# A hybrid attention layer on one core: scores negated at their source, rope DMAs and k copies reordered on ScalarE, top-k halves moved

## The chip, the core and the metric

The kernel runs on one core of one Trainium2 chip. Its time is the device time of one execution in microseconds (us); three executions of the kernel before gave 364.44, 366.65 and 367.55 us, median 366.65. Five engines run side by side and meet only at semaphores: TensorE (PE in the profile), VectorE (DVE), ScalarE (ACT), GpSimd (POOL) and SyncE (SP), which here only issues DMAs. ACT issues DMAs too; those rows are marked ACTq.

## What is computed

One decoder layer over 16 meta tokens and 512 others, so 528 positions, width 1024. All of it is float32.

```python
h = layer_norm(concat(meta, x))
qa, ka, va, ga, qi, ki, wi, cq, ckv, kpe, gb = split(h @ w_in)
# branch A: an indexer scores keys, the best 128 per row stay, 8 heads of 64
idx = sum_h relu(qi_h @ ki.T * scale_i) * wi_h ; sel = top_k(idx, 128)
la = qa @ k_sel.T * scale_a + bias[distance] ; oa = softmax(la) @ v_sel
# branch B: low-rank q and kv, 8 heads of 64, plus 32 rotary columns
q_nope, q_pe = rms(cq) @ w_uq ; k_nope, vb = rms(ckv) @ w_ukv
lb = (q_nope @ k_nope.T + rope(q_pe) @ rope(kpe).T) * scale_b, causal
ob = softmax(lb) @ vb
out = concat(oa * silu(ga), ob * silu(gb)) @ w_out
y = layer_norm(ALPHA * h + out)
```

A softmax subtracts each row's maximum before the exponential.

## The kernel before

The program is written out by hand. The function schedule() makes one list, ORDER, of stages, and each of the five engine programs walks that same list in order and does its own part of each stage. So a stage's place in the list sets its place on every engine that has work in it, and an engine never overtakes itself.

The weights come from HBM in blocks of 128 columns (raw). Stage W n makes a block's high part on ACT (wh, line 508) and its low part on POOL or DVE (wl, line 501); PE then multiplies in three passes (high by high, high by low, low by high). SP loads the raw block n+3 when the low part of block n is done. A stage J is one such product, a job, and writes one of two PSUM banks in turn: job j may start when job j-2 has been copied out. Jobs named in the steps: qn p and kn p (the 64 non-rotary columns of q and k of head pair p of branch B; kn comes in two halves), va (v of branch A), qa p and ka p (q and k of branch A; ka in two halves), tq g (three of the transposes of head g), out (the output projection).

Heads are numbered g = 0 to 15; 0 to 7 are branch B, 8 to 15 are branch A. For each head:

- S g: PE writes the scores of four row tiles into PSUM in two units, and DVE finds each row's maximum (mx; line 1025, for branch A line 1027, which also adds the bias). DVE then multiplies three, and later one, of these maxima by minus the scale (nm, line 1033).
- X g: ACT does four exponentials with bias nm (line 798), each of which also gives the row sum.
- R g: DVE takes the reciprocals, POOL scales the rows.
- TP g and tq g: PE transposes the probabilities of head g; these stages come inside head g+1.
- PV p: PE multiplies by v for a pair of heads.

In branch B, each pair's q_b holds 64 copied rows and 32 rotary rows. The rotary rows were computed earlier for all heads (qpe), and two DMAs of 64 KB, issued by ACT right behind its copy of q_b, bring them in (line 716). PE waits for both before S of the pair's first head (qpe_in). ACT's copies of kn and ka out of PSUM are lines 720 and 739; DVE's parts of them are lines 931 and 937.

The top-k is 14 rounds of two halves each (pick() puts them into ORDER as TOPK r half): a long half over the row tile of 512 keys and a short one over the three smaller tiles. DVE does them between other work of heads 0 to 7. After the last of them DVE makes the mask (MASK), and then copies qa 0 out (line 909).

## Time and profile before

| what | value |
|---|---|
| median of three runs | 366.65 us |
| lowest, highest | 364.44, 367.55 us |
| profiled execution, its time | 364.95 us |
| its span in the trace | 363.1 us |
| PE busy | 335.2 us (92%) |
| DVE, ACT, POOL busy | 241.4, 173.8, 160.2 us |
| granted TensorE clock, mean | 0.996 |

The time of an execution is the span plus what lies around it, here 1.85 us. "Idle before" in a row is how long that engine stood still before the instruction, and what ended the wait. A matmul's end is modelled, so its start is the better mark; a gap on PE is a wait that a row names.

### The profile page before, as it was taken

The page shows a single profiled execution, that of the slowest core. Times are in us where ns is not written, and L with a number is a line of the kernel's source. Part 1 is how long each engine was busy: PE and PEld are TensorE (multiplying, and loading weights), DVE is VectorE, ACT ScalarE, POOL GpSimd, SP SyncE. Part 2 cuts the span into 40 slices and gives each one's busy share as a digit, 9 for nine tenths or more (in the row PEclk, how much of TensorE's full clock was granted, in tenths as well). Part 3 has the DMA queues.
Part 4 walks back from the last instruction along what each step waited for, and adds up shares of the span by engine and source line. Part 5 has one row for each costly group of instructions (what it writes and reads, how often), then busy time and mean ns, then how long its engine had stood idle before and what let it go on. Part 6 is the DMA issues. An engine that isn't in the chain of part 4 may idle for free.

```text
span 363.1 us, 6163 instructions
## 1 busy us (share of the span) xinstructions
PE 335.2 (92%) x2155; PEld 277.1 (76%) x2155; DVE 241.4 (66%) x654; ACT 173.8 (48%) x382; POOL 160.2 (44%) x140
## 2 busy tenths in 40 slices
PE   1699999999999979999999999999989899999991
PEld 1488887888788748886968877887868688987981
DVE  5762221297766989888986796667767775533566
ACT  4674644542743354557344554654666542622230
POOL 3342999766341612346304450742233222550464
PEclk9999999999999999999999999999999999999998
DMA  7463433249211231013000140421312220130023
GB/s 265 157 214 138 133 108 104 81 170 290 69 60 58 86 105 58 16 58 116 18 16 0 60 146 3 145 89 58 92 28 89 88 81 11 58 117 0 2 116 118
DMA packets 11566, 32.87 MB, mean 91 GB/s; under 512 B 2392, under 2 KB 2392, under 8 KB 11536
## 3 DMA queue, kind: packets, MB, share of 16 engines
q1 hardware_dynamic: 8944, 27.08, 21.8%
q10 hardware_dynamic: 2592, 5.40, 4.9%
q8 instruction: 18, 0.29, 0.4%
q14 instruction: 12, 0.10, 0.1%
HBM read 29.83 MB, written 4.81 MB: 95 GB/s over the span
## 4 chain that ended last, share of the span: by engine, by line
PE 69%; DVE 10%; ACT 8%; issue 7%; DMA 2%; POOL 2%; SPq 0%; ACTq 0%; DVEq 0%; POOLq 0%
PE ps_j L1153 44%; PE ps_s L1342 5%; PE ps_o L1393 5%; PE ps_s L1309 2%; ACT pr L798 2%; DMA res<-in_x 2%; POOL wl L501 2%; PE ps_j L1195 2%; DVE pr L1027 2%; PE ps_t L1363 1%; ACT ks L739 1%; ACT wh L508 1%; PE ps_s L1350 1%; PE ps_t L1368 1%; PE ps_j L1206 1%
## 5 line engine op out<-in xcount | busy, mean ns | idle before, releaser
L501 POOL TENSOR_TENSOR wl<-raw,wh 128x1024 fp32r<-128x1024 f32 (+2 forms) x33 | 77.3, 2348 | 92.8 <-ACT wh L508 92.7
L1153 PE MATMUL ps_j<-hh,wh 128*128 128x512 f32 (+2 forms) x224 | 79.4, 354 | 1.4 <-DVE qs L909 1.3
L1153 PE MATMUL ps_j<-hl,wh 128*128 128x512 f32 (+2 forms) x224 | 77.8, 347 | 0.0
L1153 PE MATMUL ps_j<-hh,wl 128*128 128x512 f32 (+2 forms) x224 | 77.7, 347 | 0.0
L631 POOL TENSOR_SCALAR pr<-pr,rden 128x528 f32<-128x528 f32 (+1 forms) x64 | 33.7, 546 | 60.8 <-DVE rden L1042 60.8
L1153 PEld LDWEIGHTS ps_j<-hh,wh 128*128 128x128 f32 (+1 forms) x224 | 41.9, 187 | 11.0 <-issue 5.5
L1153 PEld LDWEIGHTS ps_j<-hh,wl 128*128 128x128 f32 (+1 forms) x224 | 41.8, 187 | 5.4
L1153 PEld LDWEIGHTS ps_j<-hl,wh 128*128 128x128 f32 (+1 forms) x224 | 41.8, 187 | 5.4 <-issue 0.2
L508 ACT ACTIVATE wh<-raw 128x1024 fp32r<-128x1024 f32 (+2 forms) x35 | 35.9, 1039 | 4.4 <-DMA raw<-in_weights 2.8
L1153 PE MATMUL ps_j<-wh,hh 128*128 128x256 f32 (+1 forms) x112 | 32.1, 286 | 2.4 <-ACT k_b L720 1.3
L1153 PE MATMUL ps_j<-wl,hh 128*128 128x256 f32 (+1 forms) x112 | 31.4, 280 | 0.0
L1153 PE MATMUL ps_j<-wh,hl 128*128 128x256 f32 (+1 forms) x112 | 31.3, 280 | 0.0
L798 ACT ACTIVATE pr<-pr,nm 128x528 f32<-128x528 f32 (+3 forms) x32 | 18.0, 564 | 22.5 <-DVE nm L1033 22.5
L798 ACT ACTIVATE pr<-ps_s,nm 128x528 f32<-128x528 f32 (+3 forms) x32 | 16.9, 540 | 19.5 <-DVE nm L1033 19.5
L996 DVE MATCH_REPLACE8 iw<-top,iw 128x512 f32<-128x512 f32 (+3 forms) x56 | 26.2, 475 | 0.0
L992 DVE MAX8 top<-iw 128x8 f32<-128x512 f32 (+3 forms) x56 | 24.5, 478 | 0.0
L1153 PEld LDWEIGHTS ps_j<-wh,hh 128*128 128x128 f32 (+1 forms) x112 | 19.6, 175 | 4.4 <-issue 2.5
L1342 PE MATMUL ps_s<-k_b,q_b 96*128 96x240 f32 (+4 forms) x80 | 22.2, 404 | 0.0
L909 DVE SCALAR_TENSOR_TENSOR qs<-ps_j,qs 64x512 fp32r<-64x512 f32 x16 | 11.0, 689 | 15.9 <-ACT qs L700 15.6
L980 DVE SCALAR_TENSOR_TENSOR iw<-ps_s,wi,iw 128x512 f32<-128x512 f32 (+3 forms) x28 | 13.5, 543 | 10.9 <-ACT ps_s L784 10.8
L1153 PE MATMUL ps_j<-wh,mbh 128*128 128x256 f32 x64 | 18.7, 292 | 1.4 <-DVE res L946 1.4
L1153 PEld LDWEIGHTS ps_j<-wh,hl 128*128 128x128 f32 (+1 forms) x112 | 19.6, 175 | 0.4
(216 smaller groups left out, 756.0 us busy)
## 6 DMA issues: line engine op xcount, KB each, us to landing
raw<-in_weights SPq DMA_DIRECT2D x37, 512.0 KB, 3.4
bias_by_distance<-bias_vector ACTq DMA_DIRECT2D x1, 2624.0 KB, 13.5
bias<-bias_by_distance ACTq DMA_DIRECT2D x8, 264.0 KB, 3.2
res<-in_x SPq DMA_DIRECT2D x4, 512.0 KB, 5.4
out<-res SPq DMA_DIRECT2D x3, 512.0 KB, 2.8
pt<-in_ln_emb_g SPq DMA_DIRECT2D x1, 512.0 KB, 5.2
pt<-in_ln_emb_b SPq DMA_DIRECT2D x1, 512.0 KB, 6.6
q_b<-qpe ACTq DMA_DIRECT2D x8, 64.0 KB, 2.0
```

The source lines that it names most:

```text
L501: eng.tensor_tensor(ring_of(False, b), raw_of(b), ring_of(True, b).bitcast(F32), ALU.subtract).then_inc(done, 1)
L508: act.activation(ring_of(True, b), raw_of(b), ACT.Copy).then_inc(w_high, 1)
L631: pool.tensor_scalar(a, a, rden[:, k, n:n + 1], 1.0, ALU.mult, ALU.mult).then_inc(scaled, 1)
L798: act.activation(dst, src, ACT.Exp, bias=nm[:, k, n:n + 1], scale=SCALE_B if g < HEADS else 1.0, accum_out=den[:, k, n:n + 1]).then_inc(e_ ...
L909: dve.scalar_tensor_tensor(out=qs[HD:P, n % 2, e, :], in0=bank[HD * e:HD * e + HD, :], scalar=SCALE_A, in1=qs[0:HD, n % 2, e, :].bitcast(F32),
L980: dve.scalar_tensor_tensor(out=iw[:, s], in0=ps_s[:, s], scalar=wi[:, i, h:h + 1], in1=iw[:, s] if h else ci[:, NQ - P * (i + 1):NQ], op0= ...
L992: dve.max(top8[:, i, :], iw[:, IOFF[i]:IOFF[i] + P * (i + 1)]).then_inc(done, 1)
L996: dve.match_replace(out=a, in_to_replace=top8[:, i, :], in_values=a, imm_value=TAKEN).then_inc(done, 1)
L1027: last = dve.tensor_tensor_reduce(pr[:, k, POFF[i]:POFF[i] + NK[i]], src, bias[:, g - HEADS, T - NK[i]:T], 1.0, -3e38, ALU.add, ALU.max, m ...
L1153: last = pe.matmul(dst, a, b, start=n == 0 and part[0], stop=n == count - 1 and part[1])
L1342: pe.matmul(dst, q_b[:, e, i * P:(i + 1) * P], k_b[:, e, a:b], start=True, stop=b <= c0)
L1393: last = pe.matmul(ps_o[HD * e:HD * e + HD, q0:NQ], v[0:r, j, c:c + HD], pt[0:r, e, CO[j]:CO[j] + NQ - q0], start=j == 0, stop=j == 4)
```

## The change

Five things.

1. Scores are negative from the start. The copies of qn, the rotary product and the copies of qa carry a factor of minus the scale, the bias table is negated and the mask value is positive. DVE now finds a row's minimum (mn), which is the exponential's bias as it stands; the exponential's scale is -1. The 32 small multiplications (nm) are gone, and so are the DVE's own waits ahead of them. The semaphores s_max and s_neg become one, s_min, counted per tile.
2. The rotary product's two multiplications by the tables become scalar_tensor_tensor, and DVE's copy of q_b a tensor_scalar.
3. The two rope DMAs of a pair become a stage of their own, QPE p, behind both halves of kn p.
4. The weight block that came right behind qn 0 comes behind va 0 0, the first va job. In heads 9, 11 and 13 the first half of ka comes ahead of X instead of behind it.
5. Top-k halves: one more in heads 2 and 6, and none behind R 7, where there were two.

```diff
-    job("qn", 0)
-    job("kn", 0, 0)
-    job("kn", 0, 1)
+    job("qn", 0, extra=0)
+    job("kn", 0, 0, extra=0)
+    job("kn", 0, 1, extra=0)
+    order.append(("QPE", 0))
...
-        order += [("S", g), ("X", g)]
+        order.append(("S", g))
+        if g > HEADS and g % 2 and more:
+            job(*jobs.pop(0), extra=0)
+        order.append(("X", g))
...
         if g < HEADS and g % 2 == 0:
-            pick(2 if g == 4 else 1)
+            pick(1 if g == 0 else 2)
         if g == HEADS - 1:
-            pick(2)
             assert not halves
...
             job(*j, extra=int(j[0] == "out"))
+            if j[0] == "kn" and j[2]:
+                order.append(("QPE", j[1]))
...
-                        act.activation(q_b[0:HD, 0, :], bank[0:HD, :], ACT.Copy).then_inc(job_act, 1)
-                        act.wait_ge(rope_t, n // 2 + 1)
-                        for e in range(2):
-                            r = 32 * ((2 * n + e) % 4)
-                            act.dma_start(q_b[HD:HD + 32, e, :], qpe[r:r + 32, n // 2, :]).then_inc(qpe_in, 16)
+                        act.activation(q_b[0:HD, 0, :], bank[0:HD, :], ACT.Copy, scale=-SCALE_B).then_inc(job_act, 1)
...
+                elif stage == "QPE":
+                    n = arg[0]
+                    act.wait_ge(rope_t, n // 2 + 1)
+                    if n:
+                        act.wait_ge(s_mm, 4 * n)
+                    for e in range(2):
+                        r = 32 * ((2 * n + e) % 4)
+                        act.dma_start(q_b[HD:HD + 32, e, :], qpe[r:r + 32, n // 2, :]).then_inc(qpe_in, 16)
...
-                        act.wait_ge(s_neg, 2 * g + (1 if n < 3 else 2))
+                        act.wait_ge(s_min, 4 * g + (3 if n < 3 else 4))
...
-                        act.activation(dst, src, ACT.Exp, bias=nm[:, k, n:n + 1],
-                                       scale=SCALE_B if g < HEADS else 1.0,
+                        act.activation(dst, src, ACT.Exp, bias=mn[:, k, n:n + 1], scale=-1.0,
...
-                        dve.tensor_tensor(tmp[:, 1, :], tmp[:, 1, :], sin_sb[:, META:T], ALU.mult).then_inc(rope_m, 1)
+                        dve.scalar_tensor_tensor(out=tmp[:, 1, :], in0=tmp[:, 1, :], scalar=-SCALE_B,
+                                                 in1=sin_sb[:, META:T], op0=ALU.mult, op1=ALU.mult).then_inc(rope_m, 1)
...
-                        dve.wait_ge(s_max, 4 * g + n)
-                        dve.tensor_scalar(nm[:, k, n0:n], mx[:, k, n0:n], -SCALE_B if g < HEADS else -1.0, None,
-                                          ALU.mult).then_inc(s_neg, 1)
```

PE's instructions stand in the same order as before; only the semaphores it waits on carry other names. Three places where the other engines' order changes:

ACT at the first pair (q_b, k_b: q and k of branch B; v_a: v of branch A; wh: a weight block's high part). Before, then of the change:

```order
L712 ACTIVATE q_b<-ps_j 64x512
L716 DMA q_b<-qpe 32x512 x2
L508 ACTIVATE wh<-raw 128x8x128
L720 ACTIVATE k_b<-ps_j 64x264 x2
L727 ACTIVATE v_a<-ps_j 128x256
```

```order
L715 ACTIVATE q_b<-ps_j 64x512
L719 ACTIVATE k_b<-ps_j 64x264 x2
L747 DMA q_b<-qpe 32x512 x2
L726 ACTIVATE v_a<-ps_j 128x256
L511 ACTIVATE wh<-raw 128x8x128
```

The DMAs and the weight block moved behind the k_b copies, the block behind v_a too.

ACT at the second pair, in head 1; heads 3 and 5 have the same. Before, then of the change:

```order
L798 ACTIVATE pr,den<-ps_s,nm 128x400
L712 ACTIVATE q_b<-ps_j 64x512
L716 DMA q_b<-qpe 32x512 x2
L727 ACTIVATE v_a<-ps_j 128x256
L720 ACTIVATE k_b<-ps_j 64x264 x2
L809 ACTIVATE pt<-ps_t 128x512
```

```order
L805 ACTIVATE pr,den<-ps_s,mn 128x400
L715 ACTIVATE q_b<-ps_j 64x512
L726 ACTIVATE v_a<-ps_j 128x256
L719 ACTIVATE k_b<-ps_j 64x264 x2
L747 DMA q_b<-qpe 32x512 x2
L815 ACTIVATE pt<-ps_t 128x512
```

The DMAs moved from the head of the q, v and k copies to their end, ahead of the copies of the transposes (pt).

DVE in head 7, from the row maxima or minima (mx, mn) to the copy of qa 0 (qs); top and iw are the top-k's. Before, then of the change:

```order
L1025 TENSOR_REDUCE mx<-ps_s 128x1
L1033 TENSOR_SCALAR nm<-mx 128x1
L992 MAX top<-iw 128x8 x3
...
L1042 RECIPROCAL rden<-den 128x1
L992 MAX top<-iw 128x8
L996 MATCH_REPLACE iw<-top,iw 128x512
L992 MAX top<-iw 128x8 x3
...
L1002 TENSOR_SCALAR mask<-iw 128x128
...
L909 SCALAR_TENSOR_TENSOR qs<-ps_j,qs 64x512 x2
```

```order
L1033 TENSOR_REDUCE mn<-ps_s 128x1 x4
L1001 MAX top<-iw 128x8 x3
...
L1047 RECIPROCAL rden<-den 128x1
L1011 TENSOR_SCALAR mask<-iw 128x128
...
L915 SCALAR_TENSOR_TENSOR qs<-ps_j,qs 64x512 x2
```

A long and a short half went from between the reciprocals and the mask to heads 2 and 6.

## Rows read from the trace of the kernel before

**Rows 1.** The profile's page: span, and busy time of each engine.

```profile
span 363.1 us, 6163 instructions
PE 335.2 (92%) x2155; PEld 277.1 (76%) x2155; DVE 241.4 (66%) x654; ACT 173.8 (48%) x382; POOL 160.2 (44%) x140
```

**Rows 2.** Waits of PE from 118 us on: total, times, longest.

```profile
PE ps_j L1195 <- ACT ks L739: 2.2, 2, 1.1
PE ps_j L1153 <- DVE res L946: 1.4, 2, 0.7
PE ps_j L1153 <- ACT k_b L720: 1.3, 1, 1.3
PE ps_j L1153 <- DVE qs L909: 1.3, 1, 1.3
PE ps_j L1153 <- DVE q_b L927: 0.7, 1, 0.7
```

**Rows 3.** Timeline (start, us, instruction, idle before) of ACT at the first pair.

```profile
132.75 0.59 ACT L712 ACTIVATE q_b<-ps_j 64x512 f32<-64x512 f32 x1 [1.23 <-PE ps_j L1153]
132.76 1.22 ACTq L716 DMA_DIRECT2D q_b<-qpe  x2
...
135.05 0.64 ACT L720 ACTIVATE k_b<-ps_j 64x264 f32<-64x264 f32 x2
```

**Rows 4.** Timelines of DVE, ACT and PE between S 0 and S 1.

```profile
139.99 0.54 DVE L996 MATCH_REPLACE8 iw<-top,iw 128x384 f32<-128x384 f32 x1
140.67 1.27 DVE L1025 TENSOR_REDUCE mx<-ps_s 128x1 f32<-128x528 f32 x3
...
143.60 0.21 ACT L798 ACTIVATION_READ_ACCUMULATOR pr<-ps_s,nm 128x1 f32 x1
144.12 0.37 PE L1342 MATMUL ps_s<-k_b,q_b 96*128 96x240 f32 x1
```

**Rows 5.** Timelines of ACT and PE at the second pair, up to S 2.

```profile
148.90 0.51 ACTq L716 DMA_DIRECT2D q_b<-qpe  x1
149.44 0.62 ACTq L716 DMA_DIRECT2D q_b<-qpe  x1
152.54 0.38 ACT L720 ACTIVATE k_b<-ps_j 64x264 f32<-64x264 f32 x1 [0.44 <-PE ps_j L1153]
153.79 0.37 PE L1342 MATMUL ps_s<-k_b,q_b 96*128 96x240 f32 x1
```

**Rows 6.** Line 716's DMAs, issue to landing: all eight; the third pair's.

```profile
DMA to landing us min/median/max: 1.9/2.0/3.6
...
DMA to landing us min/median/max: 2.7/2.8/2.9
```

**Rows 7.** Timelines of DVE and ACT around a bias DMA, in head 12.

```profile
275.98 0.15 DVE L1033 TENSOR_SCALAR nm<-mx 128x1 f32<-128x1 f32 x1
276.17 0.33 ACTq L647 DMA_DIRECT2D bias<-bias_by_distance  x1
...
277.13 0.61 ACT L798 ACTIVATE pr<-pr,nm 128x400 f32<-128x400 f32 x1
```

**Rows 8.** Timeline of DVE: idle in head 2, then top-k and mask behind R 7.

```profile
163.25 0.56 DVE L1051 COPY pt<-ps_t 128x384 f32<-128x384 f32 x1 [0.70 <-PE ps_t L1372]
...
211.77 0.67 DVE L992 MAX8 top<-iw 128x8 f32<-128x512 f32 x1
...
215.50 1.04 DVE L1002 TENSOR_SCALAR mask<-iw 128x128 bf16<-128x128 f32 x4
```

**Rows 9.** Timelines of ACT and DVE in head 13: the ka copies.

```profile
286.52 3.24 ACT L739 ACTIVATE ks<-ps_j 64x264 fp32r<-64x264 f32 x8
...
287.40 3.66 DVE L937 TENSOR_TENSOR ks<-ps_j,ks 64x264 fp32r<-64x264 f32 x8 [0.59 <-ACT ks L739]
```

**Rows 10.** Timelines of DVE and POOL in head 14.

```profile
294.72 1.51 DVE L1033 TENSOR_SCALAR nm<-mx 128x3 f32<-128x3 f32 x1
...
293.79 2.41 POOL L501 TENSOR_TENSOR wl<-raw,wh 128x1024 fp32r<-128x1024 f32 x1 [5.31 <-ACT wh L508]
```

More of the change, by code:

```diff
@@ L50 @@
 SCALE_W = HEADS ** -0.5
-MASKED = -float(2.0 ** 100)
+MASKED = float(2.0 ** 100)
 FUTURE = -1e38
@@ L325, in build @@
         ones = sb("ones", [P, P])
-        mx = sb("mx", [P, 2, 4])
-        nm = sb("nm", [P, 2, 4])
+        mn = sb("mn", [P, 2, 4])
         den = sb("den", [P, 2, 4])
@@ L427, in build @@
         s_mm = sem("s_mm")
-        s_max = sem("s_max")
-        s_neg = sem("s_neg")
+        s_min = sem("s_min")
         e_done = sem("e_done")
@@ L487, in slot_free @@
             if SLOT[b] >= RING:
-                eng.wait_ge(s_neg, 4 * HEADS)
+                eng.wait_ge(s_min, 8 * HEADS)
         def high_made(eng, b):
@@ L700, in _ @@
                             act.activation(qs[0:HD, n % 2, e, :], bank[HD * e:HD * e + HD, :], ACT.Copy,
-                                           scale=SCALE_A).then_inc(job_act, 1)
+                                           scale=SCALE_A if kind == "qi" else -SCALE_A).then_inc(job_act, 1)
                     elif kind == "gate":
@@ L753, in _ @@
                         w = (512, VECW - 512)[n]
-                        act.activation(vec_sb[:, 512 * n:512 * n + w], vec_bank(n), ACT.Copy).then_inc(vec_cp, 1)
+                        act.activation(vec_sb[:, 512 * n:512 * n + w], vec_bank(n), ACT.Copy, scale=-1.0).then_inc(vec_cp, 1)
                     act.wait_ge(vec_cp, 2)
@@ L909, in _ @@
                             dve.scalar_tensor_tensor(out=qs[HD:P, n % 2, e, :], in0=bank[HD * e:HD * e + HD, :],
-                                                     scalar=SCALE_A, in1=qs[0:HD, n % 2, e, :].bitcast(F32),
+                                                     scalar=SCALE_A if kind == "qi" else -SCALE_A,
+                                                     in1=qs[0:HD, n % 2, e, :].bitcast(F32),
                                                      op0=ALU.mult, op1=ALU.subtract).then_inc(job_dve, 1)
@@ L918, in _ @@
                         dve.stream_shuffle(tmp[:, 1, :], bank, SWAP).then_inc(job_dve, 1)
-                        dve.tensor_tensor(tmp[:, 0, :], bank, cos_sb[:, META:T], ALU.mult).then_inc(job_dve, 1)
+                        dve.scalar_tensor_tensor(out=tmp[:, 0, :], in0=bank, scalar=-SCALE_B, in1=cos_sb[:, META:T],
+                                                 op0=ALU.mult, op1=ALU.mult).then_inc(job_dve, 1)
                         dve.wait_ge(job_dve, BY_DVE[j + 1])
-                        dve.tensor_tensor(tmp[:, 1, :], tmp[:, 1, :], sin_sb[:, META:T], ALU.mult).then_inc(rope_m, 1)
+                        dve.scalar_tensor_tensor(out=tmp[:, 1, :], in0=tmp[:, 1, :], scalar=-SCALE_B,
+                                                 in1=sin_sb[:, META:T], op0=ALU.mult, op1=ALU.mult).then_inc(rope_m, 1)
                         dve.wait_ge(rope_m, n + 1)
@@ L926, in _ @@
                             dve.wait_ge(s_mm, 4 * n)
-                        dve.tensor_copy(q_b[0:HD, 1, :], bank[HD:P, :]).then_inc(job_dve, 1)
+                        dve.tensor_scalar(q_b[0:HD, 1, :], bank[HD:P, :], -SCALE_B, None, ALU.mult).then_inc(job_dve, 1)
                     elif kind == "kn":
@@ L1020, in _ @@
                         dve.wait_ge(s_mm, 2 * g + u + 1)
-                        n0 = n
                         for i in tiles:
@@ L1024, in _ @@
                             if g < HEADS:
-                                last = dve.tensor_reduce(mx[:, k, n:n + 1], src, AX_X, ALU.max)
+                                last = dve.tensor_reduce(mn[:, k, n:n + 1], src, AX_X, ALU.min)
                             else:
                                 last = dve.tensor_tensor_reduce(pr[:, k, POFF[i]:POFF[i] + NK[i]], src,
-                                                                bias[:, g - HEADS, T - NK[i]:T], 1.0, -3e38,
-                                                                ALU.add, ALU.max, mx[:, k, n:n + 1])
-                            last.then_inc(s_max, 1)
+                                                                bias[:, g - HEADS, T - NK[i]:T], 1.0, 3e38,
+                                                                ALU.add, ALU.min, mn[:, k, n:n + 1])
+                            last.then_inc(s_min, 1)
                             n += 1
-                        dve.wait_ge(s_max, 4 * g + n)
-                        dve.tensor_scalar(nm[:, k, n0:n], mx[:, k, n0:n], -SCALE_B if g < HEADS else -1.0, None,
-                                          ALU.mult).then_inc(s_neg, 1)
                 elif stage == "R":
@@ L1335, in _ @@
                         else:
-                            pe.wait_ge(s_neg, 2 * (g - 1) + u + 1)
+                            pe.wait_ge(s_min, 4 * (g - 1) + (3, 4)[u])
                         for i in tiles:
```

## Prediction, made before the changed kernel ran

> **What bounds the kernel.** I read the page first: PE is busy 335.2 of 363.1 us, no other engine over 66% [rows 1]. So time is gained only where PE stands still, and lost wherever it is made to. The list of PE's waits behind the first 118 us, the stretch that the change touches, is short [rows 2]: 2.2 us for the ka copies, 1.4 us for out copies (0.7 each), 1.3 us for the copy of k_b, 1.3 us for the copy of qa 0, and 0.7 us for DVE's copy of q_b, which the change leaves alone. The 6.2 us of the first four are the ceiling of every gain. PE has no wait at all for a rope DMA, and PE's own order stays. So each part is priced by what it does to a gap of PE; the timelines round each gap show the slack.
>
> **Part 1, the nm multiplications go.** Each stood between a row maximum and the exponential that ACT waits for. Mostly that is not on PE's path. The exception is head 14: one nm took 1.51 us, since it ran beside a POOL subtraction from 293.79 to 296.20 and ended right behind it [rows 10]; undisturbed, an nm takes 0.15 us [rows 7]. Behind it on DVE stand the last maximum and the copy of the first out job, for which PE then waits 0.7 us [rows 2]. About 1.35 us of DVE time goes at that place, more than the gap, so **-0.7**. The second out wait, in head 15, hangs on ACT behind weight copies that follow that head's exponentials; they start about 0.15 us earlier without nm: **-0.15**, with 0 and -0.7 as its ends. The added forms are one-for-one: a scalar_tensor_tensor for a tensor_tensor, a tensor_scalar for a copy, of the same shape and the same PSUM bank. I take 0; no row shows the new pair, and if each q_b copy cost 0.2 us more PE would pay it only at the first pair, where DVE's q_b copy already ends PE's wait of 0.7 us [rows 2]. A fixed scale in an exponential costs what another does: 0.
>
> **Part 2, first pair.** ACT issued two DMAs and made a weight block before it copied k_b, at 135.05 [rows 3]; PE waited 1.3 us for that copy [rows 2]. Now the k_b copy follows the q_b copy, which ended at 133.34, and is done at about 133.7, before PE wants the bank. The 1.3 us go at that spot. What is late next: DVE. Its top-k halves last until 140.53, and it began S 0's maxima at 140.67 [rows 4]; S 0 comes 1.3 us earlier, but DVE does not. The third exponential's sum was read at 143.60 to 143.81 and PE entered S 1 at 144.12 [rows 4], with 0.3 us to spare. Without nm and with the maxima starting at about 140.5, that exponential ends about 0.33 us earlier, at 143.48, and PE, ready at 142.8, must wait until 143.55. So of 1.3 us some 0.75 come back as a wait at S 1: **-0.55**, ends -0.3 and -1.3. The rope DMAs are now issued when kn 0 is done, at 134.4 and 134.95; with 2.0 us to land they are in at 137.0, and S 0 wants them at 137.3. With 3.6 us [rows 6] S 0 would start at 138.6, which the wait at S 1 mostly hides: 0. The weight block (for qn 1) is made 3.6 us later, on ACT, POOL and in SP's next load; PE needs it at about 146, it is done by about 141.5: 0.
>
> **Part 3, the other three pairs.** This is the part that costs. PE's order is kn p, then 1.25 us of transposes, then S: ACT saw the last kn done at 152.54 and PE began S 2 at 153.79 [rows 5]; the two later pairs, in heads 3 and 5, repeat it to within 0.02 us. Before, the DMAs went out at 148.90 and 149.44, over 4 us ahead [rows 5]. Now ACT first waits for kn's last half. The second DMA goes out 0.54 us behind the first, and lands L later, so S starts at 152.54 + 0.54 + L, which is L - 0.71 behind its old place. With L = 2.04 that is 1.33 us, for the second and fourth pair. The third pair's DMAs had 2.7 to 2.9 us, beside a weight load which is still under way at the new place too [rows 6]; I take 2.5, between it and the undisturbed 2.0, so 1.8 us. Sum **+4.5**; ends: L = 1.9 everywhere gives 3.6, L = 3.6 everywhere 8.7. Nothing hides it: PE has no gap worth 0.4 us between 136 and 218 us to give back [rows 2].
>
> Does ACT really hold the DMA until kn is done? The rows on bias DMAs say so: at 276.17 one goes out, with no wait of its own, 0.04 us after the last nm that ACT's queue waits for (275.98 + 0.15) and while its exponentials run on to 277.7 [rows 7]. So a DMA passes running work but no open wait ahead of it; the rope DMAs at 148.90 kept to the same. The Trainium skill states it otherwise (Advanced Engine Details and Errata, Sequencer and Instruction Queues): an engine instruction is pushed into a queue, waits for its semaphores there, and the sequencer reads on. By that rule the DMAs would leave before kn is done, and this part would cost 0. It is the first rival below.
>
> The Trainium skill also gives a local DMA a fixed 2.0 us plus its bytes over 436 GB/s and tells authors to issue early and wait late (DMA: Bandwidth & Descriptors, Anatomy of one DMA, Rules for kernel authors). It speaks against this move; an estimate from that page alone is 2.15 us to land and 4.3 us for the three pairs, where the rows' sum is 4.5.
>
> **Part 4, ka ahead of the exponentials.** In heads 11 and 13 PE waits 1.1 us each to write tq, because the first ka half is copied behind the exponentials: ACT 286.52 to 289.76 for both halves, DVE from 287.40 [rows 9]. In the new place the first half is copied from about 283.2 on ACT and 284.7 on DVE and done by 286.5, while tq comes at 288.2. The exponentials start 0.5 us later, and their scaled rows are wanted one head later: 0. **-2.2**. Head 9 has no such wait: 0.
>
> **Part 5, top-k halves.** Behind R 7 a long and a short half take 211.77 to 215.4 [rows 8], then mask and qa's copy, for which PE waits 1.3 us [rows 2]. With 3.7 us less ahead of it the copy waits for ACT's instead, and is done at about 215.3, before 217.1 when PE wants it: **-1.3**. The halves go to heads 2 and 6, 1.4 us each. DVE stood idle for 0.7 us in head 2 behind its top-k [rows 8], and for more in head 6, and gets at least 0.3 us a head from nm and further time from PE's later S: 0, with +0.3 as the other end. In heads 3 to 5 halves only trade places.
>
> **Sum.** -0.7 - 0.15 - 0.55 + 4.5 - 2.2 - 1.3 = -0.4 us. Against the profiled execution, 364.95 us, that is 364.5. The median of the runs shown is 1.7 us above it; against the median I forecast **366.2 us**: no change that can be measured. About 1%, 3.7 us, is what a measurement of this kernel can tell from no change.
>
> **Rivals.**
> - The DMAs are not held (above). Then part 3 is 0 and the sum is -4.9: **361.8 us**, faster by 1.3%. For it: the Trainium skill's rule. Against it: [rows 7], and the same in the other six bias DMAs without a wait of their own and in the first rope DMA of each later pair: they left 0.04 to 0.13 us behind the last nm. Chance 0.11.
> - More than 3.7 us gained although they are held: the S 1 wait doesn't come, L is 1.9, and gaps below what the list counts close with nm. Ends of the terms: -0.7 - 0.7 - 1.3 + 3.6 - 2.2 - 1.3 = -2.6, and it would take 1.1 us beyond that: 362.5. Chance 0.07.
> - Slower: rope DMAs land late. L was 3.6 us once of eight [rows 6]. If the new places meet weight loads or other transfers, L = 3.6 in each of the three heads makes 8.7 us of part 3, a sum of +3.8: **370.4 us**. It decides from L of about 3.6 us on average; the third pair's 2.8 speaks for it, the 2.0 of two others against. Chance 0.1.
> - DVE becomes the bound in heads 2 to 6 with the halves moved there: the copy of q_b or k_b would come late in three heads by up to 0.7 us, +2: 368.2. It was never waited for there before. Chance 0.04, within 1%.
>
> The forecast, with its smaller variants, has 0.68. Chances: faster by over 1% 0.18, within 1% 0.72, slower 0.10. The range takes in the first rival's edge and the ends of part 3 short of its worst: 362.0 to 369.0.
>
> **What would show it.** In the changed profile, PE's waits should name the rope DMA (q_b<-qpe) three times, at S 2, S 4 and S 6, with 1.3 to 2 us each, and a wait of about 0.7 us at S 1 for ACT's exponential. The waits for ks and qs should be gone, the two for out copies one, and smaller. The rope DMAs should be issued with the last k_b copy of their pair. The forecast is wrong if S 2, S 4 and S 6 show no wait, if those waits pass 2.5 us, or if PE waits for DVE in heads 2 to 6.

## The result, and the profile after

| kernel | median us | lowest, highest | runs |
|---|---|---|---|
| before | 364.97 | 363.74, 367.55 | 20 |
| after | 369.06 | 364.34, 373.53 | 20 |

After over before is 1.0052, 95% interval 1.0028 to 1.0075: slower by half a percent. By the medians it is 4.1 us, 1.1%. The two differ because the ratio leaves out runs over 1.5% above the fastest of their kernel, and the median has all 20. The forecast of 366.2 us was 2.9 us too low, and 369.06 us lies 0.06 us outside its range. Taken as a change it missed by more: -0.4 us was forecast and +4.1 us came. The forecast hung on the median of three executions, 366.65 us, which 20 executions of the same kernel put at 364.97, so the base was 1.7 us too high and hid that much of the miss. The wide spread is the first thing to explain. The runs of the changed kernel stand on steps, and each step has its own granted clock:

| mean granted clock of the run | runs | us | mean |
|---|---|---|---|
| 0.994 to 0.996 | 4 | 364.34 to 365.94 | 365.1 |
| 0.991 | 2 | 366.30, 366.32 | 366.3 |
| 0.985 to 0.987 | 7 | 367.64 to 370.51 | 369.0 |
| 0.977 to 0.978 | 7 | 371.88 to 373.53 | 372.7 |

The kernel before has one such step, and seldom: of its 23 runs in the first comparison below, 19 had a clock of 0.992 or more, and four 0.990, with 367.1 to 367.4 us; none was lower. The changed kernel was at 0.991 or less in 16 of 20. So there are two things to explain: what it costs at full clock (365.1 us, against 364.4, the median of before's 19 runs at 0.992 or more: no change to speak of, as the sum had it), and a loss of clock that comes and goes from run to run.

The profiled execution of the changed kernel took 366.30 us, one of the two at 0.991. Its page, to be held against [rows 1]; the last row shown is the granted clock in 40 slices, in tenths:

```profile
span 364.4 us, 6134 instructions
...
PE 336.8 (92%) x2155; PEld 277.9 (76%) x2155; DVE 231.6 (64%) x622; ACT 173.9 (48%) x382; POOL 160.5 (44%) x140
...
PEclk9999999999999999999999899999999999999998
```

DVE has 32 instructions and 9.8 us less busy time. Those 32 are the nm; they lasted 11.3 us in all, partly side by side with their neighbours. PE has the same 2155 matmuls and yet 1.6 us more busy time: the same products ran more slowly somewhere, and one slice in the middle shows an 8.

PE's waits from 118 us on answer to [rows 2] (us in total, times, longest):

```profile
PE ps_s L1347 <- DMA q_b<-qpe: 5.1, 3, 2.0
PE ps_j L1158 <- ACT k_b L719: 1.1, 2, 0.7
PE ps_j L1158 <- DVE res L959: 1.0, 3, 0.4
PE ps_s L1347 <- ACT v_a L726: 0.5, 1, 0.5
PE ps_j L1158 <- ACT pt L732: 0.4, 1, 0.4
```

All that was to go is gone: ks 2.2, qs 1.3, the 1.3 for k_b, and the 1.4 for out copies but for a 0.4 that now names pt. (The 0.7 in k_b's row is the wait at the first pair that stood as q_b's before, with both copies done at about the same time; its other 0.4 was a wait of 0.2 for v_a. The row for res was there before, with 1.1 us.) What came is 5.1 us for the rope DMAs, in three waits, and 0.5 us at S 0, the row that names v_a; e6_first_pair_alone below says what that is. The sum of all of PE's gaps from 30 us on is 9.1 us in both traces.

Then the stretches of one of these waits, at S 6. Timeline of ACT, to be held against [rows 5] (start, us, instruction, idle before):

```profile
196.43 0.38 ACT L719 ACTIVATE k_b<-ps_j 64x264 f32<-64x264 f32 x1 [0.53 <-PE ps_j L1158]
196.49 1.16 ACTq L747 DMA_DIRECT2D q_b<-qpe  x2
```

The chain of waits through the same place (start, us, what):

```profile
196.49 0.51 ACTq L747
...
197.03 2.07 DMA q_b<-qpe
199.10 0.25 issue
199.34 1.13 PE ps_s L1347 x4
```

And PE's timeline there:

```profile
197.29 0.55 PE L1200 MATMUL ps_j<-ident,pr 128*128 128x128 f32 x3
199.34 1.13 PE L1347 MATMUL ps_s<-k_b,q_b 96*128 96x240 f32 x4 [1.50 <-DMA q_b<-qpe]
...
201.50 1.63 PE L1347 MATMUL ps_s<-k_b,q_b 96*128 96x400 f32 x2
...
203.35 0.41 PE L1158 MATMUL ps_j<-wh,hl 128*128 128x256 f32 x1
...
205.06 0.28 PE L1158 MATMUL ps_j<-wl,hh 128*128 128x256 f32 x1
```

The DMAs leave 0.06 us behind the start of ACT's last k_b copy, not before. The second lands at 199.10, and PE starts S 6 0.25 us later. The 256-column products behind it read 0.41 us at 203.35 and 0.28 us at 205.06: same line, same shape. Busy time by stretch says why (us, then busy time of PE, weight loads, DVE, ACT, POOL, then the granted clock, DMA share, GB/s):

```profile
195.00:199.00 4.00, 2.53 (x21) 1.89 (x20) 3.01 (x11) 2.38 (x7) 0.10 (x1) 1.00 0.13 33
199.00:201.00 2.00, 1.66 (x9) 1.30 (x10) 0.89 (x6) 0.73 (x1) 1.19 (x1) 1.00 0.00 0
201.00:204.00 3.00, 3.00 (x13) 2.06 (x12) 1.98 (x5) 0.89 (x3) 1.15 (x1) 0.51 0.25 63
204.00:206.00 2.00, 2.00 (x17) 2.00 (x16) 1.96 (x8) 1.31 (x6) 0.56 (x1) 0.87 0.45 176
```

PE stood for most of 197.8 to 199.3; from 201.1 to 204.5 it was granted half its clock (1.2 instead of 2.4 GHz). Followed matmul by matmul, S 6 runs 4.5 us later than before, and the products behind the slow stretch 6.1 us later: it cost 1.6 us by itself. In the trace of before the clock falls only at 360.1 us, 4.8 us behind PE's last matmul, where it costs PE nothing:

```profile
355.00:360.00 5.00, 0.27 (x3) 0.07 (x1) 4.47 (x8) 0.29 (x1) 2.87 (x2) 1.00 0.24 96
360.00:365.00 5.00, 0.00 (x0) 0.00 (x0) 0.68 (x2) 0.00 (x0) 0.00 (x0) 0.51 0.31 116
```

All 13 traces end so. Of them the eight with a mean clock of 0.992 or more have no slow stretch ahead of PE's last matmul, and the five with 0.991 or less have one each. So a mean of 0.991 or less is taken below as the sign of a fall; what differs between 0.992 and 0.996 in these traces is only where that last stretch begins.

That is one slow stretch, and it makes one step of the table above. The others fit: a run of span s whose mean clock is d under 0.995 had PE at half clock for 2·s·d longer, and loses half of that, s·d. For 0.986 that is 368 · 0.009 = 3.3 us (measured 369.0 - 365.1 = 3.9), for 0.9775 it is 6.5 us (measured 7.6), for 0.991 it is 1.5 us (measured 1.2). This is an estimate: only one run of this kernel was traced, and the end of the span alone moves the mean by up to 0.004.

### The profile page after: what moved, and what is told of

It reads as the page before. It is cut to its first block, busy times and chain, and to the rows that moved or that the text cites. A ratio compares the mean times of both kernels' runs of the same rounds, so it can differ in the third digit from the quotient of the medians.

```text
span 364.4 us, 6134 instructions
## 1 busy us (share of the span) xinstructions
PE 336.8 (92%) x2155; PEld 277.9 (76%) x2155; DVE 231.6 (64%) x622; ACT 173.9 (48%) x382; POOL 160.5 (44%) x140
## 4 chain that ended last, share of the span: by engine, by line
PE 79%; DVE 5%; DMA 5%; issue 4%; ACT 4%; POOL 2%; SPq 0%; ACTq 0%; DVEq 0%; POOLq 0%
PE ps_j L1158 51%; PE ps_s L1347 6%; PE ps_o L1398 5%; PE ps_s L1355 3%; PE ps_s L1314 2%; DMA res<-in_x 2%; POOL wl L504 2%; DMA q_b<-qpe 2%; PE ps_j L1200 2%; PE ps_t L1368 1%; PE ps_s L1357 1%; PE ps_t L1373 1%; ACT pr L805 1%; PE ps_j L1211 1%; PE ps_j L1216 1%
## 5 line engine op out<-in xcount | busy, mean ns | idle before, releaser
L1347 PE MATMUL ps_s<-k_b,q_b 96*128 96x240 f32 (+4 forms) x80 | 23.5, 422 | 5.6 <-DMA q_b<-qpe 5.1
L805 ACT ACTIVATE pr<-ps_s,mn 128x528 f32<-128x528 f32 (+3 forms) x32 | 16.9, 539 | 20.8 <-DVE mn L1033 20.8
L805 ACT ACTIVATE pr<-pr,mn 128x528 f32<-128x528 f32 (+3 forms) x32 | 18.0, 565 | 10.7 <-DVE mn L1035 10.6
L1033 DVE TENSOR_REDUCE mn<-ps_s 128x1 f32<-128x528 f32 (+3 forms) x32 | 14.1, 501 | 11.0 <-PE ps_s L1351 11.0
```

What stands on the lines that cost most here:

```text
L805: act.activation(dst, src, ACT.Exp, bias=mn[:, k, n:n + 1], scale=-1.0, accum_out=den[:, k, n:n + 1]).then_inc(e_done, 1)
L1033: last = dve.tensor_reduce(mn[:, k, n:n + 1], src, AX_X, ALU.min)
L1347: pe.matmul(dst, q_b[:, e, i * P:(i + 1) * P], k_b[:, e, a:b], start=True, stop=b <= c0)
```

## Where the time went: the rope DMAs

The theory at this point: the parts gain what was forecast, the three waits for rope DMAs take it back at full clock, and PE's standing at those waits is what lets the clock fall. The rival: the clock falls with something else in the changed kernel (the new order of loads, the negated data), and the waits have nothing to do with it.

**e1_rope_early**: the changed kernel with the rope DMAs of the last three pairs back behind the q_b copy. (rope_in(act, n) is a helper with what stage QPE did: its waits and the pair's two DMAs.)

```diff
@@ kind == "qn" on ACT
                         act.activation(q_b[0:HD, 0, :], bank[0:HD, :], ACT.Copy, scale=-SCALE_B)...
+                        if n:
+                            rope_in(act, n)
@@ stage == "QPE" on ACT
-                    n = arg[0]
-                    ...
+                    if arg[0] == 0:
+                        rope_in(act, 0)
```

> The changed kernel with one edit: the rope DMAs of pairs 1 to 3 go out right behind ACT's q_b copy again, as before the change (pair 0 keeps its new place). Theory A (the rope DMAs are held behind kn, PE waits for them at S 2, S 4 and S 6, and the TensorE clock falls to 1.2 GHz behind such a wait in many executions): the three waits (1.57, 1.99, 1.50 us) are gone, and no stretch at half clock is left but the one at the end of the program. Gain over the kernel before = its gaps 9.1 us less the 4.0 that remain = 5.1 us: about 360 us, ratio 0.986, with runs within 2 us of each other. Rival B (the clock falls because of something else in the change, such as the negated scores or the moved top-k): the three waits are gone too, but stretches at half clock stay in most runs, and the runs spread over several us.

Measured: 359.14 us (358.04 to 360.1, 6 runs, all at a clock of 0.993 or 0.994), ratio 0.9841, interval 0.9803 to 0.9879. So this one move turns 4.1 us of loss into 5.5 us of gain. It is 9.9 us faster than the changed kernel, of which the three waits are only 5 to 6. (The two come from different comparisons; each held against its own runs of before, the difference is 9.6 us.) PE's waits from 118 us on:

```profile
PE ps_j L1163 <- DVE res L964: 1.0, 3, 0.4
PE ps_j L1163 <- ACT k_b L729: 0.7, 1, 0.7
```

No wait is over 0.7 us, and the clock does not fall ahead of PE's last matmul. The third pair's second DMA took 3.8 us to land here (166.93 to 170.69), longer than any in the changed kernel, and PE did not wait for it: it had gone out early enough.

**e2_rope_late_alone**: the kernel before, with nothing of the change but these three pairs' DMAs behind kn.

```diff
@@ schedule()
             job(*j, extra=int(j[0] == "out"))
+            if j[0] == "kn" and j[2]:
+                order.append(("QPE", j[1]))
@@ kind == "qn" on ACT (the DMAs of pair 0 stay)
-                        act.wait_ge(rope_t, n // 2 + 1)
-                        for e in range(2): ...
+                        if n == 0: ...
...
+                elif stage == "QPE" and arg[0]: ...
```

> The kernel before with one edit: the rope DMAs of pairs 1 to 3 behind kn. Theory A: three waits of 1.5 to 2.0 us for the rope DMA on PE, 5 to 6 us, less up to 1.3 us that the wait for qa's copy gives back since DVE catches up with the top-k; plus 1.7 us for each stretch of 3.4 us at half clock, none to four in a run. So 369 to 371 us without such a stretch, 370 to 377 us in all. Rival B: 369 to 371 us in every run, with no stretch at half clock.

Measured: 372.03 us (370.12 to 373.24, 6 runs), ratio 1.0191, interval 1.0151 to 1.0231; five of the six runs at a clock of 0.990 or less. The profiled execution:

```profile
PE ps_s L1351 <- DMA q_b<-qpe: 5.8, 3, 2.3
PE ps_j L1204 <- ACT ks L741: 2.1, 2, 1.1
```

5.8 us of waits, and 7.35 us by the medians. Its clock, too, falls behind one of the waits: S 4 starts at 177.21, the half clock begins at 179.0.

```profile
175.00:178.00 3.00, 1.01 (x6) 0.75 (x5) 2.60 (x13) 1.04 (x3) 0.90 (x2) 1.00 0.19 51
178.00:182.00 4.00, 4.00 (x17) 2.75 (x16) 2.31 (x7) 0.89 (x3) 0.00 (x0) 0.63 0.00 0
```

This kernel has none of the negation and none of the other moves. So none of that is needed for the fall. (By the length of the waits alone the run was expected at 369 to 371 us; the one run at 0.992 took 370.12.)

**e4_rope_between**: the changed kernel with the DMAs of the last three pairs between the two halves of kn instead of behind both. Pair 0 keeps its place, though the expectation has all four pairs.

```diff
-            if j[0] == "kn" and j[2]:
+            if j[0] == "kn" and not j[2]:
                 order.append(("QPE", j[1]))
```

> The changed kernel with the rope DMAs behind the first half of kn, ahead of its second (all four pairs). ACT sees the first half of kn done 0.4 to 1.0 us before the second. The wait at S is issue of the first DMA + 0.54 + time to land - start of S, so each of the three waits shrinks by that much, to 0.5 to 1.5 us; sum of the gain 2 to 2.5 us. Theory A: shorter waits let the clock fall less often, so the median gains more than the waits alone: 363 to 365 us. Rival (a DMA does not wait for the copies ahead of it, and the lateness has another cause): the waits stay as they are.

Measured: 365.91 us (362.42 to 370.05, 12 runs), ratio 1.0018, interval 0.9984 to 1.0051; four runs had a clock of 0.992 or more, with 362.4 to 364.4 us; the other eight had 0.988 or less. At S 2 and S 6 PE now waits 0.6 us; at S 4, where the second DMA took 2.5 us to land and not 2.0 or 2.1, it still waits 1.6 us:

```profile
PE ps_s L1347 <- DMA q_b<-qpe: 1.6, 1, 1.6
...
PE ps_s L1347 <- ACT pt L732: 0.6, 1, 0.6
PE ps_s L1347 <- ACT pt L730: 0.6, 1, 0.6
```

The rows of 0.6 us name ACT's copies of pt, but S has no wait for these in the program, and it began 0.24 and 0.25 us behind the second DMA's landing, as in the changed kernel; so these waits are for the DMA too. Against PE's own work the DMAs went out 0.9, 0.4 and 0.9 us earlier. That takes away about half of the waiting (5.1 to 2.8 us) and a third of the loss (3.2 of 9.9 us), and leaves falls in 8 of 12 runs. So it is no remedy for the clock: one wait of 1.6 us was left, and the clock is still unsteady. The next runs test that by itself.

## What makes the clock fall: one wait, filled, or longer

**e3_filler**: the changed kernel with dummy products on PE while it would wait at S 2, S 4 and S 6. The sums are overwritten and nobody reads them. (p is the pair; the wait on e_done makes sure that the previous head's exponentials have read the bank.)

```diff
@@ stage == "S" on PE, ahead of pe.wait_ge(qpe_in, ...)
+                        if p:
+                            pe.wait_ge(e_done, 4 * (g - 1) + 3)
+                            for _ in range(4 if p == 2 else 3):
+                                pe.matmul(ps_s[:, SOFF[3]:SOFF[3] + 240], q_b[0:HD, 0, 3 * P:4 * P],
+                                          k_b[0:HD, 0, 0:240], start=True, stop=True)
```

> The changed kernel with one addition: while PE waits for the rope DMAs at S 2, S 4 and S 6 it runs 3, 4 and 3 products of 64 x 240 on the rows of q_b and k_b that are already there, into the PSUM region that S overwrites next (their results are not used). They take about 1.5, 2.0 and 1.5 us. Theory A: S starts when it did, within 0.5 us, but PE was not idle, so the clock does not fall: all runs at 364.5 to 366.5 us, granted clock at 0.994 or more. If the clock falls because of the sequence of work and not because of PE's idleness, runs spread from 364 to 373 us as those of the changed kernel do.

Measured: 366.11 us (364.35 to 369.47, 12 runs), ratio 1.0034, interval 1.0001 to 1.0067; two of 12 runs at 0.991 or less (369.0 and 369.5 us), where the changed kernel had 16 of 20. S starts no sooner (the ten other runs took 365.8 us on average, the changed kernel's four at full clock 365.1), PE does more work, and the median is 2.9 us lower. At S 2 three products were too few: 0.7 us of wait was left.

**e9_one_wait**: e1_rope_early with one late pair, the third.

```diff
-                        if n:
+                        if n in (1, 3):
                             rope_in(act, n)
...
-                    if arg[0] == 0:
-                        rope_in(act, 0)
+                    if arg[0] in (0, 2):
+                        rope_in(act, arg[0])
```

> e1_rope_early with the rope DMAs of the third pair alone behind the last kn copy: PE waits once, at S 4, for about 2.0 us (as in the changed kernel), at S 2 and S 6 it doesn't. Against e1_rope_early's 359.1 us the wait costs 2.2 us. If PE's clock falls because PE stood at such a wait, at most one stretch of half clock (1.7 to 2 us) is added ahead of the last jobs, and only in part of the runs: the runs lie at 361.3 and 363.1 us, median 361.3 to 363.2. Rival (the clock falls by chance, with PE's high load over the run, whatever the waits): e1's six runs had no fall, so none or as many as the kernel before's (4 of 23), median 361.3. Second rival (three waits are needed, one does nothing): as the rival, no run above 362.5.

Measured: 363.60 us (361.66 to 364.8, 12 runs), ratio 0.9946, interval 0.992 to 0.9972. The three runs at 0.992 or more took 361.66 to 362.13 us, 2.5 to 3 us over e1_rope_early; the nine others, at 0.985 to 0.989, took 362.70 to 364.80. One wait is enough. The median is above the range expected (361.3 to 363.2), since a fall can last longer than 3.4 us: in the profiled execution it lasted 6.8 us and cost 3.2 us. PE there:

```profile
171.75 0.55 PE L1205 MATMUL ps_j<-ident,pr 128*128 128x128 f32 x3
174.16 1.13 PE L1352 MATMUL ps_s<-k_b,q_b 96*128 96x240 f32 x4 [1.86 <-DMA q_b<-qpe]
```

```profile
172.00:174.00 2.00, 0.30 (x3) 0.06 (x1) 1.83 (x8) 1.04 (x3) 0.95 (x3) 1.00 0.29 82
174.00:175.00 1.00, 0.84 (x4) 0.77 (x5) 0.00 (x0) 0.00 (x0) 0.00 (x0) 1.00 0.00 0
175.00:178.00 3.00, 3.00 (x11) 1.76 (x9) 0.93 (x2) 0.00 (x0) 0.00 (x0) 0.57 0.00 0
178.00:182.00 4.00, 4.00 (x19) 3.81 (x18) 3.79 (x15) 2.20 (x8) 0.54 (x1) 0.50 0.00 0
```

**e11_one_wait_filled**: the same kernel, and four dummy products in that one wait. This is the sharpest pair of the study, since nothing but what PE does in the wait differs.

```diff
@@ e9_one_wait, stage == "S" on PE, ahead of pe.wait_ge(qpe_in, ...)
+                        if p == 2:
+                            pe.wait_ge(e_done, 4 * (g - 1) + 3)
+                            for _ in range(4):
+                                pe.matmul(... 64x240 ..., start=True, stop=True)
```

> e9_one_wait with four products of 64x240 (their sums are overwritten, none is read) in the place of PE's wait at S 4, once the exponential ahead has freed the bank. S 4 starts when it did, so runs at full clock lie at 361.3 to 362.1 us as the three fastest of e9_one_wait. If PE's standing still is what makes the clock fall, the stretch at half clock behind S 4 is gone and the median is 361.9 us, with no more than 2 of 12 runs at a clock under 0.990 (9 of 12 in e9_one_wait). Rival (it is the late transfer, or the load at that place, whatever PE does meanwhile): the falls stay, most runs under 0.990, median 363.6 us.

Measured: 362.06 us (361.37 to 362.72, 6 runs), ratio 0.9929, interval 0.9905 to 0.9953; all six runs at 0.992 or more, where e9_one_wait had three of 12. The counts are clear, though there were six runs and not the 12 expected; the gain in time, 1.5 us by the medians, is not clear of noise by itself, since the two intervals overlap. PE there (x8, because each of the four dummy products shows as two instructions):

```profile
171.97 0.55 PE L1205 MATMUL ps_j<-ident,pr 128*128 128x128 f32 x3
172.44 1.89 PE L1334 MATMUL ps_s<-k_b,q_b 64*128 64x240 f32 x8
174.26 1.16 PE L1357 MATMUL ps_s<-k_b,q_b 96*128 96x240 f32 x4
```

```profile
172.00:174.00 2.00, 2.00 (x13) 1.69 (x11) 1.93 (x8) 1.04 (x3) 1.15 (x3) 1.00 0.39 123
174.00:175.00 1.00, 1.00 (x5) 0.68 (x4) 0.10 (x2) 0.00 (x0) 0.00 (x0) 1.00 0.00 0
175.00:178.00 3.00, 3.00 (x20) 2.27 (x19) 1.49 (x4) 0.18 (x1) 0.00 (x0) 1.00 0.00 0
```

S 4 starts 2.29 us behind the transposes' start here and 2.41 us there, so it starts as late as in e9_one_wait; with PE busy meanwhile, the clock stays. The rival (it is the transfer, or the load at that place) is out.

**e10_one_long_wait**: e9_one_wait with the wait made longer. ACT issues the second DMA only when the first has landed.

```diff
@@ rope_in, e9_one_wait
             for e in range(2):
+                if n == 2 and e == 1:
+                    act.wait_ge(qpe_in, 32 * n + 16)
                 act.dma_start(...)
```

> e9_one_wait with ACT waiting until the first rope DMA of the third pair has landed before it issues the second: one wait of PE at S 4 of about 4.0 us (2.0 more), nothing else moved. If the length of the wait makes the fall of the clock more likely, the stretch at half clock stands behind S 4 in most runs: 359.1 + 4.2 + 1.8 = 365.1 us. Rival (the wait's length doesn't matter or the clock falls by chance): 363.3 us in most runs, a share of falls as in e9_one_wait or the kernel before.

Measured: 367.36 us (366.01 to 368.81, 12 runs), ratio 1.0064, interval 1.0041 to 1.0088; all 12 runs at 0.985 or less. The wait was 3.5 us instead of 1.9, and the clock fell every time:

```profile
PE ps_s L1354 <- DMA q_b<-qpe: 3.5, 1, 3.5
```

```profile
172.00:174.00 2.00, 0.00 (x0) 0.00 (x0) 1.50 (x6) 0.12 (x1) 0.58 (x2) 1.00 0.12 34
174.00:175.00 1.00, 0.00 (x0) 0.00 (x0) 0.00 (x0) 0.92 (x3) 0.00 (x0) 0.89 0.27 66
175.00:178.00 3.00, 2.55 (x6) 1.88 (x7) 0.00 (x0) 0.00 (x0) 0.00 (x0) 0.50 0.00 0
178.00:182.00 4.00, 4.00 (x16) 2.75 (x15) 2.20 (x6) 1.10 (x4) 0.00 (x0) 0.55 0.00 0
```

Here the clock fell at 174.8, while PE still stood, and S 4 began slow. The time is 2.3 us above the sum of 365.1. By the starts of the same matmuls, held against e1_rope_early's trace, the wait cost 3.7 us where 4.2 was reckoned and the slow stretch 3.1 us where it was 1.8. With these the sum is 365.9 us, near the traced execution's 366.22. The other 1.1 us up to the median were not traced. The Trainium skill (TensorE: Matmul & The Clock Gate, What's actually happening) says that half the clock is the default and activity is what releases the full one. These traces agree: the clock fell behind or in PE's waits, and it shows the levels 0.50 and 1.00 and nothing between but averages over a change.

Side by side, with the kernel before and the four kernels of the next section for scale:

| kernel | PE's waits at S 2, S 4, S 6, us | runs at 0.991 or less |
|---|---|---|
| before | none (longest elsewhere 1.3) | 4 of 23; over all the comparisons 14 of 82 |
| e5, e6, e7, e8 | none (longest elsewhere 1.3) | 1 of 6, 0 of 10, 1 of 8, 1 of 10 |
| e1_rope_early | none of note | 0 of 6 |
| e11_one_wait_filled | one, filled | 0 of 6 |
| e3_filler | three, filled but for 0.7 | 2 of 12 |
| e9_one_wait | 1.9 | 9 of 12 |
| e4_rope_between | 0.6, 1.6, 0.6 | 8 of 12 |
| after | 1.6, 2.0, 1.5 | 16 of 20 |
| e2_rope_late_alone | 2.3, 2.0, 1.5 | 5 of 6 |
| e10_one_long_wait | 3.5 | 12 of 12 |

So falls are not confined to the kernels with long waits: without one, and without a filled one, they came in 17 of 122 runs. A long wait makes them the rule. What starts them in the 17 was not traced.

## The other parts, each alone on the kernel before

**e5_negation_alone**: the scales, the mask and bias sign and the minima as in the change, the order as before.

```diff
-                        act.wait_ge(s_neg, 2 * g + (1 if n < 3 else 2))
+                        act.wait_ge(s_min, 4 * g + (3 if n < 3 else 4))
...
-                        dve.wait_ge(s_max, 4 * g + n)
-                        dve.tensor_scalar(nm[:, k, n0:n], mx[:, k, n0:n], -SCALE_B if g < HEADS else -1.0, None,
-                                          ALU.mult).then_inc(s_neg, 1)
```

> The kernel before with the negation alone (minima, bias mn, scales of -1 and -SCALE_B); every instruction keeps its old place, nm is gone. Prediction's part 1: PE's wait for the first out copy of head 14 (0.7 us) goes, the one of head 15 shrinks by 0.15, the added forms cost 0: -0.85 us, some 364 us, ratio 0.998. PE's waits for ks (two of 1.1), qs (1.3) and k_b (1.3) stay, no wait for a rope DMA, no stretch at half clock before the last jobs. Rival (the new forms cost DVE time that PE pays, and with it some of the excess of the changed kernel): waits for q_b grow by 0.2 us or more and the run is 1 us or more slower, 366 us.

Measured: 361.59 us (361.28 to 364.57, 6 runs), ratio 0.993, interval 0.9896 to 0.9965. That is 3.1 us of gain where 0.85 was expected. The out wait went as forecast; but other waits shrank too:

```profile
PE ps_j L1198 <- ACT ks L742: 1.6, 2, 0.8
PE ps_j L1156 <- ACT k_b L723: 1.3, 1, 1.3
...
PE ps_j L1156 <- DVE qs L913: 0.4, 1, 0.4
```

ks 2.2 to 1.6 and qs 1.3 to 0.4, against [rows 2]. The likely reason is that both hang on DVE and on exponentials, which come earlier in every head without nm (11.3 us of DVE over 32 of them, 0.35 each on average, not the 0.15 of the shortest). Together with the out waits these make 2.4 of the 3.1 us. No wait for q_b grew: the new forms cost what the old did (DVE's q_b copy 0.69 us in both, the two products of the rotary step 0.68 and 1.59 us before, 0.67 and 1.59 here).

**e6_first_pair_alone**: the rope DMAs of pair 0 behind kn 0, weight block 20 behind the first va job.

```diff
-    job("qn", 0)
-    job("kn", 0, 0)
-    job("kn", 0, 1)
+    job("qn", 0, extra=0)
+    job("kn", 0, 0, extra=0)
+    job("kn", 0, 1, extra=0)
+    order.append(("QPE", 0))
```

> The kernel before with only the first pair's order changed: the two rope DMAs of pair 0 behind kn 0, weight block 20 behind the first va job. Part 2 of the prediction: PE's wait of 1.3 us for the k_b copy goes, and some of it comes back at S 1 as a wait for the exponential. nm is still there, so that comes back nearly whole: 1.0 us at S 1, gain 0.3 us, 364.4 us, ratio 0.999. Rival (S 0 waits for the late DMA more than S 1 would, as in one look where it landed 2.45 us behind its issue): wait of 0.5 us for the DMA at S 0, which shortens the one at S 1 by as much, time unchanged.

Measured: 364.23 us (363.0 to 365.62, 10 runs), ratio 0.9978, interval 0.995 to 1.0006, 0.5 us against before's 364.73: in size as forecast, though too small to be told from nothing. The 1.3 us for k_b are gone, and two waits came:

```profile
136.66 1.13 PE L1349 MATMUL ps_s<-k_b,q_b 96*128 96x240 f32 x4 [0.50 <-ACT v_a L732]
142.75 0.47 PE L1349 MATMUL ps_s<-k_b,q_b 96*128 96x240 f32 x1 [0.30 <-ACT pr L805]
```

The second rope DMA landed at 136.46; S 0 began 0.2 us behind it. The row names v_a's copy, which ended at about the same time, but S 0 has no wait for that copy in the program. In e1_rope_early S 0 began at 136.27, again 0.2 us behind the landing, while v_a's copy ran until 136.55. So the wait is for the DMA. It shortens the wait at S 1, as the rival in the expectation had it.

**e7_ka_ahead_alone**: the first ka half ahead of the exponentials in heads 9, 11 and 13.

```diff
-        order += [("S", g), ("X", g)]
+        order.append(("S", g))
+        if g > HEADS and g % 2 and more:
+            job(*jobs.pop(0), extra=0)
+        order.append(("X", g))
```

> The kernel before with only the first ka half of heads 9, 11 and 13 ahead of the exponentials. Part 4: PE's two waits for ks (1.1 us each) go, nothing comes in their place: -2.2 us, 362.5 us, ratio 0.994; all other waits as before. Rival (the exponentials start later and the wait moves on to tq's next reader or to the out copies): ks waits gone, a new wait of about 1 us in heads 12 or 14 and a gain of 1 us or less.

Measured: 362.37 us (361.65 to 364.81, 8 runs), ratio 0.9944, interval 0.9918 to 0.9969: 2.4 us of gain for 2.2 forecast. The ks row is gone from PE's waits and nothing has come.

**e8_topk_alone**: the two halves behind R 7 moved to heads 2 and 6.

```diff
-            pick(2 if g == 4 else 1)
+            pick(1 if g == 0 else 2)
         if g == HEADS - 1:
-            pick(2)
```

> The kernel before with only the two top-k halves behind R 7 moved to heads 2 and 6. Part 5: PE's wait for qs (1.3 us) in head 7 goes, nothing comes in its place: -1.3 us, 363.4 us, ratio 0.9965. Rival (DVE is late in head 2 or 6 with the added 1.4 us): a new wait of PE for DVE there of 0.3 to 0.7 us, gain 0.6 to 1 us.

Measured: 363.96 us (363.0 to 366.17, 10 runs), ratio 0.9983, interval 0.9953 to 1.0013: 0.8 us by the medians, not told from nothing, for 1.3 forecast. qs is gone; in its place DVE is late with a copy of q_b in head 3:

```profile
PE ps_j L1194 <- ACT ks L738: 2.2, 2, 1.1
...
PE ps_j L1152 <- DVE q_b L926: 1.1, 2, 0.7
```

The q_b row was 0.7 in one wait before [rows 2]; the second wait is 0.44 us. In the changed kernel it is missing, where nm's time is gone from DVE as well.

The four parts alone give 3.1 + 0.5 + 2.4 + 0.8 = 6.8 us; together, in e1_rope_early, they give 5.5. The difference is what e5 took of the ks and qs waits (0.6 and 0.9), which e7 and e8 take too.

## Why the prediction was wrong

The step that failed is part 3, "This is the part that costs", priced at +4.5 us with ends of 3.6 and 8.7. It is the right mechanism at the right three places, but the term is mis-sized: the rope DMAs in their late place cost 9.9 us by the medians (changed kernel against e1_rope_early), 6.0 us at full clock (365.1 against 359.1). Two things are in it.

- The waits themselves. Followed by the start of the same matmul, S 2, S 4 and S 6 cost 1.74, 2.24 and 1.75 us, together 5.7 for 4.5. L was 2.1, 2.6 and 2.1 us, close to what I took. Missing were the 0.25 us from landing to PE's start, since I let S begin at the moment of landing, and 0.06 us from the start of the last k_b copy to the first issue.
- The clock. The sum had no term for it. PE at half speed for 3.4 or 6.8 us at a time, behind waits of 1.5 to 2 us, cost 0 in the four best runs, 3.9 us in the seven in the middle and 7.6 us in the seven worst, 3.9 at the median (369.06 against 365.1).

The failure of reasoning is that I read [rows 1] and [rows 2] as time PE stands still, and took a wait to cost what it lasts. In the trace of before PE's longest wait behind 118 us is 1.3 us [rows 2], and its clock holds until PE is done; nothing in it shows what a wait of 2 us does. So the price was not to be had from these rows, but the range should have said so: every wait that the change put in was longer than any there, and a clock at 1.2 GHz behind them was a term with an unknown end above, not a zero.

The other points:

- Do DMAs wait for what stands ahead of them in ACT's list? Yes. At S 6 ACTq's issue at 196.49 is 0.06 us behind the start of the k_b copy, at the two others the same. They do pass running work: that copy ended at 196.81. The rival of DMAs that leave early (361.8 us) is out. By the Trainium skill's rule (Advanced Engine Details and Errata, Sequencer and Instruction Queues) they would have left before the copy could start. The traces do not bear that out: each time they left behind its start.
- Part 1, 0.85 us: too small by itself, 3.1 us measured alone, because I looked for nm only where PE waited for an out copy. In the changed kernel this error nearly cancels, since parts 4 and 5 take the same waits.
- Part 2, 0.55 us: 0.5 alone, which no run tells from nothing. I had 0.75 us come back, all at S 1; in the changed kernel 0.47 us came back at S 0 and 0.09 at S 1: the second DMA took 2.45 us to land, not 2.0.
- Part 4, 2.2 us: 2.4 alone.
- Part 5, 1.3 us: 0.8 alone, the whole of the qs wait in the changed kernel. "DVE becomes the bound in heads 2 to 6" is true without the negation (0.44 us), and not with it.
- Without part 3 the sum was -4.9 us, and e1_rope_early gave -5.5. That is closer than the parts deserve: part 1 was 2.3 us too small alone, and the overlap of the waits that it shares with parts 4 and 5 took over half of that back.
- The second rival's time, 362.5 us, does not follow from its own terms: 366.65 less 2.6 and 1.1 is 362.95.
- The prediction's estimate of 2.15 us to land takes the Trainium skill's fit (DMA: Bandwidth & Descriptors, Anatomy of one DMA) from a section on DMAs that GpSimd issues; these are issued by ScalarE. In the changed kernel the second DMA of a late pair took 2.14, 2.56 and 2.07 us, so two of three agree.
- The slower rival (370.4 us, 0.10) is near the measured time for a wrong reason, which is luck: it wanted L = 3.6 us in each head, and L was 2.1 to 2.6.
- What would show it: the named waits at S 2, S 4 and S 6 came as said and stayed under 2.5 us; only the 0.7 us at S 1 did not come (0.09). So by its own signs of being wrong the forecast stood. None of them took in the clock.

Open: why one run falls and the next of the same kernel does not, why a fall lasts 3.4 us in one and 6.8 us in another, and where in before's four slower runs the clock fell, since its profiled execution was none of them. Between 1 and 1.5 us of e10_one_long_wait's median isn't accounted for.

## What to carry to other kernels

A wait on the engine that bounds the kernel costs its length and then, if it is long enough, the clock behind it. Where a change puts a new wait of 1.5 us or more on a busy TensorE, price it at about twice its length until runs say otherwise (an estimate from these runs: 9.9 us in all for waits of 5.7, 4.5 for 2.0 and 8.2 for 3.7), and read each run's granted clock beside its time: steps in the times with steps in the clock are the sign. And an early DMA that hides behind more than four microseconds of other work is to stay early: this move alone stood between a change that gained 1.6% and one that lost. If such a wait can't be removed, products that nobody reads, in its place, hold the clock (e11_one_wait_filled, 1.5 us by the medians).

## What the runs showed of the hardware

- By the mean clock, TensorE fell to half clock (0.50) in 9 of 12 runs with one wait of 1.9 us amid otherwise full work, in 16 of 20 with three of 1.5 to 2 us, in 12 of 12 with one of 3.5 us, and in 17 of 122 with none above 1.3 us from 30 us on. The slow stretch began 0.4 to 1.8 us after PE had resumed (four traces), or still in the wait (e10_one_long_wait), and lasted 3.4 or 6.8 us.
- The same 256-column product reads 0.41 us in it and 0.28 us outside; a fall of 3.4 us cost 1.6 us, one of 6.8 us 3.1 to 3.2 us.
- From a DMA's landing to the start of the matmul that waited for it: 0.24 to 0.25 us, three times; at S 0 0.20 us. A rope DMA of 64 KB took 1.9 to 3.8 us from issue to landing (all 13 traces).
- A multiplication of one to three columns on DVE (nm) took 0.15 us undisturbed [rows 7], 0.35 us on average and 1.51 us beside a POOL subtraction [rows 10]. Taking out 32 of them (e5_negation_alone) gained 3.1 us, though PE never waited for one directly.
